# A two-layer hybrid decoder step on one core: where the low halves of the next weights and of the later prompt rows are made

## The chip, the core and the metric

The kernel runs on one core of one Trainium2 chip. The metric is the device time of one execution in microseconds (us); lower is better. A core has five engines that run their own instruction streams: TensorE (PE in the rows, with its weight loads as PEld), VectorE (DVE), ScalarE (ACT), GpSimd (POOL) and SyncE (SP, which here only issues DMAs). They meet through semaphores.

## The reference, cut to what matters

Two layers, each of them one mixer over 2048 prompt rows and 32 sample rows (8 sequences of 4 tokens) of width 1024, in float32:

```python
for l in range(DEPTH):                                    # DEPTH = 2
    h = rms_norm(x, norm_g[l])
    p = h @ w_in[l]                                       # 1024 x 3328, columns split as
    qa, ka, va, ga, qb, kb, vb, gb = split(p)             # 512 128 128 512 | 4 x 512
    attn = sliding-window attention of qa, ka, va with sinks   # 8 heads of 64, 2 kv heads, window 128
    ret  = rms_norm(retention of qb, kb, vb)              # 4 heads of 128, chunks of 128
    x = x + concat(silu(ga) * attn, silu(gb) * ret) @ w_out[l]
```

The outputs are x for prompt and sample, and the new key, value and retention states.

## The kernel before, in words

**Two halves in place of float32.** TensorE multiplies in float16. Each float32 factor is scaled by a power that keeps it in range and split into a high half, hi = f16(x * s), and a low half, lo = f16(x * s - hi). A product is the sum of three matmuls (hi*hi, hi*lo, lo*hi). The high half of a weight chunk is made by ACT (`w_high`, the ACTIVATE at line 1692), the low half by DVE in one instruction (`w_low`, lines 916 to 920: multiply by the scale, subtract the high half, write float16). For the rows of x it is the same: `p_high` (line 1894) on ACT, `p_low` (line 1348) on DVE.

**Stages.** A layer has four stages, named by their weights: A (attention: q, k, v and its gate, 1280 columns), B0 and B1 (retention, two heads each, 1024 columns) and O (the output product). Each stage walks over 17 steps: the sample rows and 16 tiles of 128 prompt rows. The weights of a stage lie in one of two SBUF slots, `w_a` (A, B1) and `w_b` (B0, O). While one stage runs, the weights of the next are loaded by POOL's DMAs into the other slot as float32, and its halves are written over them in place: the halves of chunk (k, c) end 512 words below where its raw values begin, so the low half of a chunk must be made before ACT may write the high half of the next one. That is the wait of `w_high` on the semaphore `w_lo` in front of line 1692. In stage A the next weights are B0's: 8 rows k of 128, each in two chunks c of 128x512.

**Stage A step by step.** Step s projects tile s on PE (three parts: q with 512 columns, k and v with 256, gate with 512) and at the same time takes tile t = s-1 through scores and softmax and tile u = s-2 through the product with the values. On PE (`a_step`, `a_work`) the order is: the first three quarters of part 0, the transposes of q and k of t, the rest of part 0, half of part 1, the scores of t (`a_S`, line 637), the rest of part 1, values product of u for kv group 0 (`a_PV`, line 677), three quarters of part 2, values product of u for group 1, the rest. On DVE (`a_step`, lines 1427 to 1488): low halves of q and k (`a_lo`, lines 1020 and 1022; the scores wait for them), landing of q (`a_land_q`, line 960), low halves of the probabilities of u, group 1 (`a_plo`, line 1053), the masks and maxima of both groups of t (line 1091), landing of k (line 976), the four mixed heads of group 0 and of group 1 (line 1166) with the small instructions of the norm of tile s woven between them, its rotation (lines 1002 to 1014), the gate (line 1034), and the low half of the probabilities of t, group 0 (`a_plo`, line 1048). The probabilities go through a transposing DMA issued by SP (`prob_T`, line 2192) before `a_PV` can use them, and there is one buffer for each group, so the masks of the next tile wait for the transpose of this one.

**Where the low halves stand.** In steps 8 to 15 of stage A DVE's `a_step` has `w_low(L, "B0", k, 0)` in the middle of the norm's small instructions and `w_low(L, "B0", k, 1)` at the end. ACT's `a_step` has `w_high(k, 0)` before it lands k and v, and `w_high(k, 1)` between the exponentials of group 0 and those of group 1.

**The prompt rows of layer 0.** The normalised rows h of tiles 1 to 16 are not all made before the first step. Tiles 1 to 7 are made in the prologue and steps 0 and 1. Tiles 8 to 16 are made late (`late_h`): in step c of 4 to 12, ACT makes the high half of tile c+4, DVE its low half (`p_low(c + 4)`, at the end of the step), and SP sends both through a transposing DMA into `hT` (`p_T`, line 2184), queued on SP behind the `prob_T` of that step. The raw rows lie in `hT` itself, at the place their transpose will take. In steps 4 to 6 DVE also takes the absolute maxima of the B0 weights (`w_absmax`, line 902), in step 6 the overall maximum, and in step 7 the scales (`w_scale`).

**POOL.** It loads weights (`load_weights`, lines 510 to 518) and reduces one column across partitions (`share_max`, line 2086). In `attend` (lines 2094 to 2105) it waits for one piece of stage A, loads the eight rows of B0's weights, and reduces the maximum in step 6. In layer 1 DVE, ACT, PE and SP run the middle steps in hardware loops; in layer 0 DVE's and ACT's steps 8 to 15 are written out, since `late_h` differs by step.

Of the kernel before, what the change touches and what calls it, by code (L numbers as in the profile page):

```python
# [197 lines left out]
def trunk(nc, x_prompt, x_sample, cache_k, cache_v, state_ret, w_in, w_out, norm_g, q_g, k_g, sinks,  # L198
          rope_ap, rope_as, rope_bp, rope_bs, mask_a, mask_s, decay, decay_s, cols, ident,
          y_p, y_s, nk_p, nv_p, nst_p, nk_s, nv_s, nst_s, mixed):  # L200
    with ExitStack() as ctx:
# [3 lines left out]
        def sem(name):  # L205
            return ctx.enter_context(nc.semaphore(name))
# [130 lines left out]
        h_planes = nc.dram_tensor("h_planes", (ROWS, 2 * D_MODEL), F16).ap()  # L337
        alone_count = sem("alone_count")

        ch_wm, ch_ws = sem("chain_w_max"), sem("chain_w_scale")  # L340
        ch_an, ch_asm, ch_amx = sem("chain_a_norm"), sem("chain_a_softmax"), sem("chain_a_mix")
        ch_ams, ch_bo, ch_om = sem("chain_a_mix_sample"), sem("chain_b_out"), sem("chain_o_scale")
# [109 lines left out]
        def x_of(n):  # L452
            return px[:, n % RING, :] if n < PRO else hx[:, :, (n - 1) * 64:n * 64]
# [405 lines left out]
        def _(v):  # L859
# [56 lines left out]
            def w_low(L, kind, k, c):  # L916

                v.wait_ge(w_hi, wparts(L, kind, k, c) + 1)
                V.scalar_tensor_tensor(out=w16(kind, k, c, 1), in0=raw(L, kind, k, c), scalar=w_gs[:, run(k, 1)],  # L919
                                       in1=w16(kind, k, c, 0), op0=ALU.mult, op1=ALU.subtract).then_inc(w_lo, 1)  # L920
# [423 lines left out]
            def p_low(n):  # L1344

                r = NS if n == 0 else P
                v.wait_ge(x_hi, n + 1)
                V.scalar_tensor_tensor(out=xh_of(n, 1)[0:r], in0=x_of(n)[0:r], scalar=py[0:r, n:n + 1],
                                       in1=xh_of(n, 0)[0:r], op0=ALU.mult, op1=ALU.subtract).then_inc(x_lo, 1)
# [52 lines left out]
            def layer(L, last):  # L1402
# [21 lines left out]
                    a_softmax(L, s - 1, 1)  # L1424
                    gate("A", L, s, 2, A_W, A_W + 2 * KV_W)

                def a_step(s, k=None):

                    t, u = s - 1, s - 2
                    if u.sample:  # L1430
# [23 lines left out]
                    if not u.sample:  # L1454
# [6 lines left out]
                        a_norm_link(s, ch, 2)  # L1461
                        a_mix_head(u, 0, 3).then_inc(a_mx, 1)
                        a_norm_link(s, ch, 3)
                        if k is not None:
                            w_low(L, "B0", k, 0)
                        a_norm_link(s, ch, 4)
                        a_norm_link(s, ch, 5)
                        a_mix_open(L, u, 1, m1)
# [10 lines left out]
                        a_rotate(L, s, ch)  # L1479
                        gate("A", L, s, 2, A_W, A_W + 2 * KV_W)  # L1480
                        a_plo(L, t, 0)
                        if k is not None:
                            w_low(L, "B0", k, 1)
                    else:
                        a_norm(s, ch)
                        a_rotate(L, s, ch)
# [4 lines left out]
                def late_h(c):  # L1491

                    if c == 0:
                        p_rstd(1)
                        p_low(4)
                        p_low(5)
                    if c == 1:
                        p_low(6)
                        p_low(7)
                    if c in (3, 4):  # L1500
                        p_rstd(c - 1)
                    if 4 <= c <= 12:
                        p_low(c + 4)

                for c in range(CVA):
                    if c < 2:
# [9 lines left out]
                        w_top(L, "B0")  # L1516
                    if c == 7:
                        w_scale(L, "B0")
                if L == 0:
                    for c in range(CVA, CVA + KT):  # L1520
                        a_step(Step(c), c - CVA)
                        late_h(c)
                else:
                    with v.Fori(0, KT // 2) as i:
                        for c in (0, 1):
                            a_step(Step(CVA + c, i), c + 2 * i)
                for c in range(CVA + KT, STEPS):
                    a_step(Step(c))

# [551 lines left out]
        def _(pool):  # L2081
# [9 lines left out]
            pool.sem_inc(st_out, 64)  # L2091
            share_max(0, "A")

            def attend(L):

                for c in range(STEPS):
                    if c == 2 and L == 0:
                        for p in range(2):
                            pool.wait_ge(h_in[p], 16 * (PRO // 2))
                    if c == 2:  # L2100
                        pool.wait_ge(dve_piece, L * PIECES + PIECE0["A"] + 1)
                    if c in (2, 3):
                        load_weights(G, "B0", L, range(4 * c - 8, 4 * c - 4))
                    if c == 6:
                        share_max(L, "B0")

            def layer(L, last):
                attend(L)
# [341 lines left out]
```

## Time and profile before

| | |
|---|---|
| runs | 1910.03, 1909.19, 1908.5 us; median 1909.19 |
| the profiled execution | 1908.13 us, of which its span is 1906.3 us |
| mean granted TensorE clock | 0.984 |
| busy share of the span | PE 93%, PEld 50%, DVE 72%, ACT 43%, POOL 4% |
| instructions | PE 11512, DVE 4744, ACT 1901, POOL 108 |
| stage A of layer 0 | about 65 to 400 us of the span |
| stage A of layer 1 | about 1005 to 1320 us |

The profile shows one execution. A group's row gives its busy time, the mean duration in ns, and the idle time of the engine before it with what ended that. A row of the timeline gives start, duration and, in square brackets, the idle time before it and its releaser. Engines overlap the tail of one instruction with the start of the next, so the time that an instruction costs its engine is the distance to the start of the next one, which is up to 0.09 us less than its duration; the chain of waits counts that distance.

### The profile page before, as it was taken

How to read it: one execution, taken by the hardware profiler on the slowest of the kernel's cores; microseconds unless marked ns; L12 is line 12 of the kernel's file. 1: busy time of each engine (PE TensorE's matmuls, PEld its weight loads, DVE VectorE, ACT ScalarE, POOL GpSimd, SP SyncE). 2: the span in 40 equal slices, each digit the busy share in tenths (PEclk: the TensorE clock that was granted, in tenths of full speed). 3: DMA queues.
4: the chain of work that ended last, by engine and by line, in shares of the span. 5: the costliest groups of instructions: out<-in, count | busy, mean ns of one | idle time of the engine just before them, and what ended most of it. 6: DMA issues, size and time to landing. Idle time of an engine off the chain costs nothing.

```text
span 1906.3 us, 35688 instructions
## 1 busy us (share of the span) xinstructions
PE 1770.3 (93%) x11512; PEld 961.3 (50%) x11512; DVE 1379.1 (72%) x4744; ACT 820.7 (43%) x1901; POOL 68.5 (4%) x108
## 2 busy tenths in 40 slices
PE   0778899999999999989998989999999999999999
PEld 0345555555555555543445555555555555555444
DVE  4768999987665666678885899998766666667442
ACT  2556566652443334432443556665344333442010
POOL 3010000000000000011001000000100000000000
PEclk9898999999999999999999999999999999999999
DMA  5874455466114311179894454554611133115774
GB/s 152 207 185 73 88 105 112 107 119 159 30 33 123 81 31 33 33 207 269 251 267 135 80 100 95 110 115 86 186 31 33 46 111 81 32 32 142 207 207 143
DMA packets 419519, 220.91 MB, mean 116 GB/s; under 512 B 360257, under 2 KB 391169, under 8 KB 419265
## 3 DMA queue, kind: packets, MB, share of 16 engines
q1 hardware_dynamic: 346336, 168.41, 36.4%
q0 software_dynamic: 9728, 35.66, 5.7%
q10 hardware_dynamic: 63360, 15.74, 4.9%
q8 instruction: 41, 0.67, 0.1%
q14 instruction: 54, 0.43, 0.1%
HBM read 88.75 MB, written 49.68 MB: 73 GB/s over the span
## 4 chain that ended last, share of the span: by engine, by line
PE 55%; DVE 23%; DMA 8%; ACT 5%; issue 4%; SPq 2%; DVEq 0%; ACTq 0%; POOL 0%
PE PB L547 23%; PE PA L547 22%; DMA r<-r 6%; DVE r L1091 2%; DVE r L1048 2%; DVE w_mx L902 1%; PE S L701 1%; PE OB L721 1%; PE S L737 1%; PE OB L728 1%; DVE mix L1166 1%; DVE r L1053 1%; DVE w_b L919 1%; ACT w_a L1762 1%; DVE w_a L919 1%
## 5 line engine op out<-in xcount | busy, mean ns | idle before, releaser
L547 PE MATMUL PB<-w_a,hT 128*128 128x512 f16 (+1 forms) x1920 | 406.1, 365 | 0.0
L547 PE MATMUL PA<-w_a,hT 128*128 128x512 f16 (+1 forms) x1920 | 401.4, 360 | 0.6 <-DVE land L1034 0.6
L547 PEld LDWEIGHTS PB<-w_a,hT 128*128 (+1 forms) x1920 | 187.0, 99 | 184.4 <-issue 18.9
L547 PEld LDWEIGHTS PA<-w_a,hT 128*128 (+1 forms) x1920 | 185.3, 98 | 177.0 <-issue 5.6
L1840 ACT ACTIVATE w_a<-land 128x1024 uint16<-128x1024 uint16 x60 | 63.4, 1057 | 294.2 <-DVE land L1206 281.9
L547 PE MATMUL PA<-w_b,r 128*128 128x512 f16 x768 | 175.6, 387 | 11.7 <-DMA r<-r 9.5
L547 PE MATMUL PB<-w_b,hT 128*128 128x512 f16 x768 | 176.0, 380 | 1.3 <-DVE r L1195 1.3
L547 PE MATMUL PA<-w_b,hT 128*128 128x512 f16 x768 | 173.7, 382 | 0.0
L547 PE MATMUL PB<-w_b,r 128*128 128x512 f16 x768 | 171.4, 379 | 2.3 <-DVE r L1313 1.1
L1762 ACT ACTIVATE r<-r,nm,unqk 128x256 f32<-128x256 f32 x192 | 112.6, 588 | 46.1 <-DVE sd L1104 46.1
L547 PEld LDWEIGHTS PA<-w_b,r 128*128 128x128 f16 x768 | 75.6, 99 | 106.8 <-DMA r<-r 11.2
L547 PEld LDWEIGHTS PB<-w_b,r 128*128 128x128 f16 x768 | 74.8, 98 | 93.2 <-DVE r L1319 2.1
L547 PEld LDWEIGHTS PA<-w_b,hT 128*128 (+1 forms) x768 | 74.9, 98 | 85.8 <-issue 4.2
L547 PEld LDWEIGHTS PB<-w_b,hT 128*128 (+1 forms) x768 | 74.7, 98 | 84.5 <-DVE r L1195 1.4
L1862 ACT ACTIVATE r<-r,minv 128x1024 f16<-128x1024 f32 (+1 forms) x34 | 39.0, 1148 | 145.5 <-DVE minv L1280 137.9
L1034 DVE SCALAR_TENSOR_TENSOR land<-land,PB 128x256 f32<-128x256 f32 (+2 forms) x50 | 25.3, 506 | 105.5 <-ACT land L1814 100.4
L1034 DVE SCALAR_TENSOR_TENSOR land<-land,PA 128x256 f32<-128x256 f32 (+3 forms) x52 | 26.7, 513 | 89.1 <-ACT land L1814 86.8
L1834 ACT ACTIVATE r<-w_a 128x1024 uint16<-128x1024 uint16 x60 | 82.1, 1368 | 20.6 <-DMA w_a<-w_a 20.6
L573 PE MATMUL PA<-w_a,hT 128*32 128x256 f16 (+1 forms) x336 | 22.0, 342 | 54.7 <-DVE w_a L919 53.8
L1319 DVE SCALAR_TENSOR_TENSOR r<-PB,mdd,r 128x512 f32<-128x512 f32 x32 | 23.9, 748 | 64.7 <-PE PB L547 64.4
L1692 ACT ACTIVATE w_b<-w_b,w_gs (+1 forms) x64 | 46.4, 725 | 23.1 <-DVE w_b L919 16.1
L1294 DVE SCALAR_TENSOR_TENSOR r<-r,minv 128x1024 f16<-128x1024 f32 (+1 forms) x34 | 43.4, 1278 | 17.2 <-ACT r L1862 17.1
(265 smaller groups left out, 2875.5 us busy)
## 6 DMA issues: line engine op xcount, KB each, us to landing
out<-r SPq DMA_DIRECT2D x40, 512.0 KB, 4.7
r<-mixed SPq DMA_DIRECT2D x32, 512.0 KB, 4.2
w_b<-in_w_in POOLq DMA_DIRECT2D x16, 512.0 KB, 8.8
mixed<-mix SPq DMA_DIRECT2D x32, 256.0 KB, 2.0
mixed<-mix SPq DMA_DIRECT2D x64, 128.0 KB, 1.8
w_a<-in_w_in POOLq DMA_DIRECT2D x16, 512.0 KB, 8.2
w_b<-in_w_out POOLq DMA_DIRECT2D x16, 512.0 KB, 7.8
r<-in_x_prompt SPq DMA_DIRECT2D x16, 512.0 KB, 4.4
```

The source lines that it names most:

```text
L547: last = nc.tensor.matmul(out[0:s.rows, 0:n], lhs, w16(ph, k, p, wpart), start=(k == 0 and part == 0 and wpart == 0), stop=(k == KT - 1 an ...
L919: V.scalar_tensor_tensor(out=w16(kind, k, c, 1), in0=raw(L, kind, k, c), scalar=w_gs[:, run(k, 1)], in1=w16(kind, k, c, 0), op0=ALU.mult, ...
L1034: V.scalar_tensor_tensor(out=th, in0=th, scalar=1.0, in1=src, op0=ALU.add, op1=ALU.mult).then_inc(dve_piece, 1)
L1048: V.scalar_tensor_tensor(out=ph16[0][:, 1, :], in0=r1[:, 1536:2560], scalar=P_TOP, in1=ph16[0][:, 0, :], op0=ALU.mult, op1=ALU.subtract).t ...
L1091: return V.tensor_tensor_reduce(out=prob_q[g][h // 2][:, h % 2 * 256:h % 2 * 256 + 256], in0=(SS, XX)[g][h // 2][:, (h % 2) * 256:(h % 2) ...
L1294: V.scalar_tensor_tensor(out=m[0:r, 1, :], in0=mxt[0:r, b, :], scalar=minv[0:r, b:b + 1], in1=m[0:r, 0, :], op0=ALU.mult, op1=ALU.subtract ...
L1319: V.scalar_tensor_tensor(out=x, in0=bank("O", s, p)[0:r, :], scalar=mdd[0:r, b:b + 1], in1=x, op0=ALU.mult, op1=ALU.add).then_inc(dve_piec ...
L1692: A.activation(w16(kind, k, c, 0), raw(L, kind, k, c), ACT.Copy, scale=w_gs[:, run(k, 1)]).then_inc(w_hi, 1)
L1762: A.activation(x, x, ACT.Exp, scale=unqk[:, 0:1], bias=nm[:, g, h:h + 1], accum_out=rsum[:, g, h:h + 1])
L1834: last = A.activation(qkT.bitcast(U16).rearrange("p (n e) -> p e n", e=2), plT, ACT.Copy)
L1840: A.activation(pl, land[:, lpar(ph, s), 0:512].bitcast(U16).rearrange("p (n e) -> p e n", e=2), ACT.Copy).then_inc(b_pl, 1)
L1862: A.activation(mh_of(s)[0:r, 0, :], mxt[0:r, b, :], ACT.Copy, scale=minv[0:r, b:b + 1]).then_inc(o_hi, 1)
```

## The change

In stage A the low halves of B0's weights (both layers) and of the late prompt tiles 8 to 16 (layer 0) leave DVE and go to POOL. There each is made by two instructions: a `tensor_scalar` that scales the raw values where they lie, and, after a wait for its own semaphore, a `tensor_tensor` that subtracts the high half and writes float16. DVE's steps 8 to 15 of layer 0 become a hardware loop as in layer 1. POOL loads the B0 weights in two groups of four rows, the second after three more pieces of stage A. The low halves of the other stages stay on DVE, and ACT's and SP's programs are unchanged.

```diff
+        w_pp = sem("w_scaled_in_place")
+        x_ps = sem("x_scaled_in_place")
...
# DVE
-                def a_step(s, k=None):
+                def a_step(s):
...
                         a_norm_link(s, ch, 3)
-                        if k is not None:
-                            w_low(L, "B0", k, 0)
                         a_norm_link(s, ch, 4)
...
                         a_plo(L, t, 0)
-                        if k is not None:
-                            w_low(L, "B0", k, 1)
...
                     if c in (3, 4):
                         p_rstd(c - 1)
-                    if 4 <= c <= 12:
-                        p_low(c + 4)
...
-                if L == 0:
-                    for c in range(CVA, CVA + KT):
-                        a_step(Step(c), c - CVA)
-                        late_h(c)
-                else:
-                    with v.Fori(0, KT // 2) as i:
-                        for c in (0, 1):
-                            a_step(Step(CVA + c, i), c + 2 * i)
+                with v.Fori(0, KT // 2) as i:
+                    for c in (0, 1):
+                        a_step(Step(CVA + c, i))
...
# POOL
+            def w_low(L, kind, k, c):
+
+                pool.wait_ge(w_hi, wparts(L, kind, k, c) + 1)
+                n = (L * KT + k) * len(CH[kind]) + c
+                x = raw(L, kind, k, c)
+                G.tensor_scalar(x, x, w_gs[:, k:k + 1], None, ALU.mult).then_inc(w_pp, 1)
+                pool.wait_ge(w_pp, n + 1)
+                G.tensor_tensor(w16(kind, k, c, 1), x, w16(kind, k, c, 0), ALU.subtract).then_inc(w_lo, 1)
+
+            def p_low(n):
+
+                pool.wait_ge(x_hi, n + 1)
+                x = x_of(n)
+                G.tensor_scalar(x, x, py[:, n:n + 1], None, ALU.mult).then_inc(x_ps, 1)
+                pool.wait_ge(x_ps, n - PRO + 1)
+                G.tensor_tensor(xh_of(n, 1), x, xh_of(n, 0), ALU.subtract).then_inc(x_lo, 1)
+
             def attend(L):
 
-                for c in range(STEPS):
-                    if c == 2 and L == 0:
-                        for p in range(2):
-                            pool.wait_ge(h_in[p], 16 * (PRO // 2))
-                    if c == 2:
-                        pool.wait_ge(dve_piece, L * PIECES + PIECE0["A"] + 1)
-                    if c in (2, 3):
-                        load_weights(G, "B0", L, range(4 * c - 8, 4 * c - 4))
-                    if c == 6:
-                        share_max(L, "B0")
+                if L == 0:
+                    for p in range(2):
+                        pool.wait_ge(h_in[p], 16 * (PRO // 2))
+                pool.wait_ge(dve_piece, L * PIECES + PIECE0["A"] + 1)
+                load_weights(G, "B0", L, range(4))
+                pool.wait_ge(dve_piece, L * PIECES + PIECE0["A"] + 4)
+                load_weights(G, "B0", L, range(4, KT))
+                if L == 0:
+                    for n in range(PRO, PRO + 3):
+                        p_low(n)
+                share_max(L, "B0")
+                if L == 0:
+                    p_low(PRO + 3)
+                for k in range(KT):
+                    for c in range(2):
+                        w_low(L, "B0", k, c)
+                    if L == 0 and PRO + 4 + k < STEPS:
+                        p_low(PRO + 4 + k)
```

Here PRO is 8, KT is 8, CVA is 8 and STEPS is 17.

## Rows read from the trace of the kernel before

**Rows 1.** The page's second part, the span in 40 slices of 47.7 us.
```profile
DVE  4768999987665666678885899998766666667442
...
PEclk9898999999999999999999999999999999999999
```
**Rows 2.** DVE's timeline (start, duration): landing of q, first instruction but three of a step.
```profile
155.34 0.75 DVE L960 SCALAR_TENSOR_TENSOR land<-PA,cs_A,qk_g 128x512 f32<-128x512 f32 x1
...
239.17 0.72 DVE L960 SCALAR_TENSOR_TENSOR land<-PA,cs_A,qk_g 128x512 f32<-128x512 f32 x1
...
328.03 0.72 DVE L960 SCALAR_TENSOR_TENSOR land<-PB,cs_A,qk_g 128x512 f32<-128x512 f32 x1
...
378.59 0.72 DVE L960 SCALAR_TENSOR_TENSOR land<-PA,cs_A,qk_g 128x512 f32<-128x512 f32 x1
...
1156.36 0.72 DVE L960 SCALAR_TENSOR_TENSOR land<-PA,cs_A,qk_g 128x512 f32<-128x512 f32 x1
...
1296.19 0.72 DVE L960 SCALAR_TENSOR_TENSOR land<-PA,cs_A,qk_g 128x512 f32<-128x512 f32 x1
```
**Rows 3.** The chain that ended last, layers 0 and 1 (start, us, what).
```profile
265.50 0.67 DVE w_b L919
...
272.50 1.20 DVE r L1348
...
1224.97 4.72 DMA r<-r
```
**Rows 4.** ACT's timeline around the two high halves of one step, layer 0.
```profile
256.67 0.71 ACT L1692 ACTIVATE w_b<-w_b,w_gs 128x512 f16<-128x512 f32 x1
...
266.25 0.72 ACT L1692 ACTIVATE w_b<-w_b,w_gs 128x512 f16<-128x512 f32 x1 [0.72 <-DVE w_b L919]
```
**Rows 5.** PE's timeline, layer 0: first part-1 matmuls of steps 14 and 15.
```profile
361.07 1.47 PE L547 MATMUL PA<-w_a,hT 128*128 128x256 f16 x12
...
377.52 1.47 PE L547 MATMUL PB<-w_a,hT 128*128 128x256 f16 x12
```
**Rows 6.** PE's timeline: the scores at the end of steps 4, 5 and 6.
```profile
177.86 0.40 PE L637 MATMUL S<-kT_hi,r 64*128 64x256 f16 x2 [4.51 <-DVE r L1022]
...
199.46 0.28 PE L637 MATMUL S<-kT_hi,r 64*128 64x256 f16 x2 [2.60 <-DVE r L1022]
...
220.60 0.40 PE L637 MATMUL S<-kT_hi,r 64*128 64x256 f16 x2 [3.00 <-DVE r L1022]
```
**Rows 7.** Windows (us, then busy PE, PEld, DVE, ACT, POOL; PEclk; DMA share; GB/s).
```profile
180.00:182.00 2.00, 2.00 (x13) 1.17 (x10) 2.00 (x11) 0.00 (x0) 0.00 (x0) 0.50 0.13 26
...
222.00:224.00 2.00, 2.00 (x18) 1.16 (x15) 2.00 (x8) 0.00 (x0) 0.00 (x0) 0.50 0.00 0
```
**Rows 8.** Waits (total us, times, longest): stretch 176 to 241, then 241 to 328.
```profile
DVE mix L1166 <- PE TK L677: 3.8, 3, 1.9
...
PE S L637 <- DVE r L1022: 3.8, 4, 1.0
```
**Rows 9.** DVE's groups by form, 241 to 410 us (busy us, mean ns).
```profile
L1048 DVE SCALAR_TENSOR_TENSOR r<-r 128x1024 f16<-128x1024 f32 x10 | 12.2, 1218 | 0.0
L919 DVE SCALAR_TENSOR_TENSOR w_b<-w_b,w_gs 128x512 f16<-128x512 f32 x16 | 11.9, 745 | 0.0
...
L1348 DVE SCALAR_TENSOR_TENSOR r<-hT,py,r 128x1024 f16<-128x1024 f32 x5 | 6.4, 1278 | 0.0
...
L1014 DVE TENSOR_TENSOR land<-r 128x80 f32<-128x80 f32 x9 | 2.1, 235 | 0.0
```
**Rows 10.** Timeline at the start of layer 1, POOL and PE.
```profile
1005.68 5.96 POOL L518 DMA_DIRECT2D w_b<-in_w_in  x8 [104.31 <-DVE r L1319]
...
1020.29 0.28 PE L587 MATMUL TK<-eye,land 32*64 32x32 f32 x4 [2.65 <-DVE land L1014]
```
**Rows 11.** SP's own timeline, layer 0: two transposing DMAs in their order.
```profile
256.11 2.67 SPq L2184 DMA_TRANSPOSE hT<-r  x1
259.73 1.32 SPq L2192 DMA_TRANSPOSE r<-r  x1
```

## The prediction

> **What bounds the kernel now.** I read the page's slices first, because the change touches only stage A, about a third of the span. DVE's digits there are 8 and 9 in layer 0 (slices 4 to 8) and again around layer 1's stage A, while in the retention stages they are 6 and 7 [rows 1]. So DVE is fullest exactly where the change takes work off it. The landings of q then give the length of a step [rows 2]. In layer 0 steps 4 to 7 take (239.17 - 155.34) / 4 = 20.96 us each, steps 8 to 12 (which have both kinds of low half) (328.03 - 239.17) / 5 = 17.77, steps 13 to 15 (weights only) (378.59 - 328.03) / 3 = 16.85. In layer 1 steps 8 to 15 take (1296.19 - 1156.36) / 8 = 17.48.
>
> What would PE need by itself? From the first part-1 matmuls of step 14 to those of step 15 it had no wait: 377.52 - 361.07 = 16.45 us at the full clock [rows 5]. That is the floor of a step.
>
> The chain says who sets each step. In layer 0 it runs through DVE, with the weight low halves (0.67 us each; the second of a step costs the same) and the row low half (1.20 us) on it [rows 3], and PE waits up to 1.0 us a step for DVE before the scores [rows 8]. In layer 1 it is a loop: masks, softmax, the first weight low half, ACT's high half and exponentials, gate, low half of the probabilities, then 4.72 us of transposing DMA [rows 3] before the next masks may use the buffer. Only the first of the two weight low halves is on that loop. Layer 0 shows the same link: ACT waited 0.72 us for DVE's `w_low` before the second high half [rows 4].
>
> Steps 4 to 6 of layer 0 have something more. PE waits 4.51, 2.60 and 3.00 us for DVE before the scores [rows 6], and behind the first and the third of them windows show a granted clock of 0.50, the lower level, 1.2 GHz [rows 7]. The waits of up to 1.0 us in steps 8 to 12 [rows 8] have no such dip behind them. DVE later pays: it waits 3.8 us in three places for PE's values product, 1.9 of them behind the longest gap [rows 8].
>
> **The change part by part.** The sum is made against the profiled execution, 1908.13 us; the median is 1.06 us above it, which I add at the end.
>
> *Row low halves leave DVE in steps 4 to 7.* 4 x 1.20 = 4.8 us off a full engine [rows 3]. The gaps of steps 5 and 6 shrink to 1.4 and 1.8 us; I take it that the clock then holds, as behind the 1.0 us gaps, and DVE's two later waits, 3.8 - 1.9 = 1.9 us [rows 8], go. Step 4 keeps a gap of 3.3 and its dip. Gain 6.7 us.
>
> *Both kinds leave DVE in steps 8 to 15, layer 0.* DVE gets back 2 x 0.67 + 1.20 = 2.54 us in five steps and 1.34 in three, 16.7 us; PE's floor lets through (378.59 - 239.17) - 8 x 16.45 = 7.8.
>
> *Layer 1.* The loop loses one low half: 8 x 0.7 = 5.6 us, under the floor's 139.83 - 131.6 = 8.2. The second one is beside the DMA, and gives nothing while the DMA covers it.
>
> *What POOL's instructions cost.* No row shows POOL at arithmetic. Nearest are DVE's single instructions over the same tiles, 0.75 us for 128x512 and 1.28 for 128x1024 [rows 9]; that is the lower end. The upper end at which POOL would still keep ACT's pace comes from ACT's two high halves: 266.25 - 0.72 - 257.38 = 8.15 us for two instructions, 4.1 each [rows 4]. I take DVE's durations for each of the two instructions, the nearest row. Then POOL works 4 x 0.75 + 2 x 1.28 = 5.56 us in a step with both kinds and 3.0 in one with weights only; its own time is hidden by 17 us of step.
>
> *What it costs DVE.* POOL now reads SBUF beside DVE. No row shows the two side by side, so the cost to DVE is between nothing and all of POOL's time. Should they share a path, DVE's instructions with two SBUF inputs are those exposed. In the 169 us from 241 to 410 fifteen groups are of that kind, from line 1048 with 12.2 us to line 1014 with 2.1 [rows 9], 72.7 us together, 0.43 of the stretch and 0.48 of what is left once the moved instructions are gone. I take 0.45 of POOL's time as lost to DVE. Steps 8 to 12: 0.45 x 5.56 = 2.50 against 2.54 won, nothing. Steps 13 to 15: 1.35 against 1.34, nothing. Layer 1: the second pair runs right behind ACT's second high half, beside the norm and the rotation, which are on the loop; 0.45 x 1.5 = 0.68 against 0.7, nothing. Steps 4 to 7: a pair of 2.56 us, but DVE is then partly in `w_absmax` with one input; half a us each, 2.0. Ends of this term: 0, and all of POOL's time added.
>
> The Trainium skill, SBUF — State Buffer, section Who interferes with whom, speaks against this change: a DVE instruction with two SBUF inputs and a GpSimd instruction that reads SBUF exclude each other for a whole instruction, whoever is second. No row here shows that. GPSIMD Engine Reference, section 3.1, gives a GpSimd `tensor_tensor` 1.96 times DVE's duration; with a `tensor_scalar` near DVE's own that makes 1.5 on average, an estimate, and the sum would be that of the second rival.
>
> *Small parts.* DVE's new loop in layer 0 adds register work; layer 1 has it and steps within 0.6 us of layer 0's; I take 0, at most 2 us in all. The four later loads of B0's weights in layer 1: all eight are issued at 1005.68 [rows 10]; four would now start when k of step 1 has landed, near 1028, and are needed in step 5, some 90 us later: hidden. Emptier DMAs at 1006 to 1020 win nothing, since PE waits there for DVE's rotation until 1020.29 [rows 10]. In layer 0 the piece has long come when the prologue's transposes release POOL. `share_max` in layer 0 stands behind `p_low(10)`, and DVE asks for it a step of 21 us later: hidden. SP's `p_T` now waits for POOL, with `prob_T` queued behind it: third rival.
>
> Sum: -4.8 - 1.9 + 2.0 = -4.7: 1903.4 us, by the median 1904.5. By itself this case reaches from 1899 to 1911.
>
> **The rivals.**
> *No contention.* POOL and DVE don't disturb each other. Then 6.7 + 7.8 + 5.6 = 20.1 us come off: 1889.1. For it: DVE is the engine in front, and PE's floor is a full us below the steps. Against: POOL's reads have to come from somewhere. Chance 0.20.
> *POOL's instructions hold DVE up for longer than the moved work took.* Place: beside `a_plo` and beside norm and rotation. Break-even is where POOL's instructions last 1.2 times DVE's. At 1.5 times: steps 8 to 12, 5 x (3.75 - 2.54) = 6.1; steps 13 to 15, 3 x (2.03 - 1.34) = 2.1; layer 1, 8 x (1.01 - 0.7) = 2.5; steps 4 to 7, 3.0 - 6.7 = -3.7. Together +7.0: 1916.2. At twice, +19: 1928. For it: nearly half of DVE's time is exposed. Chance 0.30.
> *SP is held up.* `p_T` takes 2.67 us of SP and the next `prob_T` follows at 259.73 [rows 11]. If POOL ends a row's low half 2 us later against DVE's plan than DVE did, that `prob_T` and PE's product behind it come later by as much, beyond the 1.3 us a step of room above the floor: with DVE's gain lost too, five steps at about 1.5 us, 1912. Chance 0.07.
> That the change does nothing to the moved work is excluded: the instructions are gone from DVE. Remainder 0.03.
>
> **How the numbers follow.** Forecast 0.40, rivals 0.20, 0.30, 0.07. A measurement of this kernel tells 0.2%, 3.8 us, from no change, so faster is below 1905.4. Half of the forecast's own range and a little of the second rival's lie there, with the first rival: 0.20 + 0.22 + 0.05 = 0.47. Slower, above 1913: most of the second rival, 0.30 with the third. The rest, 0.23, is no change. The range has to hold the first rival's value and the second at 1.6 times: 1888 to 1920.
>
> **What would show it right or wrong.** Landings of q in layer 0: steps 5 and 6 near 19 to 20 us, without a clock of 0.50 behind them; steps 8 to 12 near 17.7. If these are near 16.5, the first rival holds; above 18, the second. In the groups, line 1048 keeps its 1218 ns [rows 9] if nothing is shared, and it and the other two-input lines are longer on average if DVE waits inside them. POOL's `tensor_scalar` and `tensor_tensor` rows give the missing durations. A PE wait for the DMA before line 677 that grows by over 1 us in steps 8 to 12 is the third rival. The prediction is wrong in its reasons if the time moves in B0, B1 or O.

## The result, and the profile after

| | before | after |
|---|---|---|
| runs | 1902.85 to 1910.03 us, median 1908.85 (4) | 1921.85 to 1931.72 us, median 1929.95 (4) |
| the profiled execution, its span | 1908.13, 1906.3 us | 1931.28, 1929.5 us |
| mean granted clock | 0.984 | 0.978 |

The changed kernel takes 1.0102 times as long, with a 95% interval of 1.0075 to 1.0128. It is slower by about 20 us, where 1904.5 was forecast.

The slices of the page after answer to [rows 1]. POOL's digits are those that the change adds (3 to 5 in layer 0's stage A, up to 3 in layer 1's).

```profile
DVE  4768999987666666678885799999666666667442
...
POOL 3011345401000000011001002331100000000000
PEclk9798999999999999999998999999999999999999
```

DVE is as full as before, with less work to do. The landings of q, of DVE's timeline after, answer to [rows 2] (start, duration):

```profile
155.73 0.75 DVE L962 SCALAR_TENSOR_TENSOR land<-PA,cs_A,qk_g 128x512 f32<-128x512 f32 x1
...
240.34 0.72 DVE L962 SCALAR_TENSOR_TENSOR land<-PA,cs_A,qk_g 128x512 f32<-128x512 f32 x1
...
343.57 0.71 DVE L962 SCALAR_TENSOR_TENSOR land<-PB,cs_A,qk_g 128x512 f32<-128x512 f32 x1
...
397.48 0.75 DVE L962 SCALAR_TENSOR_TENSOR land<-PA,cs_A,qk_g 128x512 f32<-128x512 f32 x1
...
1175.61 0.72 DVE L962 SCALAR_TENSOR_TENSOR land<-PA,cs_A,qk_g 128x512 f32<-128x512 f32 x1
...
1319.73 0.75 DVE L962 SCALAR_TENSOR_TENSOR land<-PA,cs_A,qk_g 128x512 f32<-128x512 f32 x1
```

Steps 4 to 7 of layer 0 take (240.34 - 155.73) / 4 = 21.15 us (before 20.96), steps 8 to 12 (343.57 - 240.34) / 5 = 20.65 (before 17.77), steps 13 to 15 17.97 (before 16.85), and layer 1's steps 8 to 15 (1319.73 - 1175.61) / 8 = 18.02 (before 17.48). In us that is +0.8, +14.4, +3.4 and +4.3. The last landing comes 1319.73 - 1296.19 = 23.5 us later than before, and the span is 23.2 longer. The four stretches make 22.8 of it, most of that in the five steps with both kinds of low half. What else moved nearly cancels: step 1 of layer 1 is 6.3 us longer, steps 2 to 7 there are 1.5 shorter, and the time between the two stages A is 4.4 shorter (see One load group).

What POOL's instructions last is in POOL's groups by form over the whole span (busy us, mean ns):

```profile
L2090 POOL TENSOR_SCALAR w_b<-w_b,w_gs 128x512 f32<-128x512 f32 x32 | 55.7, 1740 | 180.0 <-ACT w_b L1683 180.0
L2092 POOL TENSOR_TENSOR w_b<-w_b 128x512 f16<-128x512 f32 x32 | 39.4, 1230 | 2.7
L2098 POOL TENSOR_SCALAR hT<-hT,py 128x1024 f32<-128x1024 f32 x9 | 26.3, 2920 | 101.4 <-ACT r L1885 101.4
L2100 POOL TENSOR_TENSOR r<-hT,r 128x1024 f16<-128x1024 f32 x9 | 19.6, 2183 | 0.7
```

A step with both kinds holds 2 x (1.74 + 1.23) + 2.92 + 2.18 = 11.0 us of POOL's work, where the prediction took 5.56.

Now the place where it costs. First POOL's timeline in step 10 of layer 0, then DVE's rows of the same time:

```profile
283.72 1.63 POOL L2092 TENSOR_TENSOR w_b<-w_b 128x512 f16<-128x512 f32 x1
292.16 1.56 POOL L2090 TENSOR_SCALAR w_b<-w_b,w_gs 128x512 f32<-128x512 f32 x1 [6.81 <-ACT w_b L1683]
293.81 1.16 POOL L2092 TENSOR_TENSOR w_b<-w_b 128x512 f16<-128x512 f32 x1
296.21 2.98 POOL L2098 TENSOR_SCALAR hT<-hT,py 128x1024 f32<-128x1024 f32 x1 [1.24 <-ACT r L1885]
299.27 2.15 POOL L2100 TENSOR_TENSOR r<-hT,r 128x1024 f16<-128x1024 f32 x1
```
```profile
284.25 1.12 DVE L1118 TENSOR_TENSOR rr<-rsum,es 128x4 f32<-128x4 f32 x1
...
292.26 0.61 DVE L883 TENSOR_TENSOR rt<-rs 128x10 f32<-128x10 f32 x1
292.99 0.15 DVE L885 TENSOR_TENSOR rt<-rt,ss 128x10 f32<-128x10 f32 x1
...
293.92 1.07 DVE L887 SCALAR_TENSOR_TENSOR rs<-rt,rs 128x10 f32<-128x10 f32 x1
...
296.60 0.95 DVE L1015 TENSOR_TENSOR land<-r 128x80 f32<-128x80 f32 x1
...
298.22 1.21 DVE L1050 SCALAR_TENSOR_TENSOR r<-r 128x1024 f16<-128x1024 f32 x1
...
299.36 2.08 DVE L1118 TENSOR_TENSOR rr<-rsum,es 128x4 f32<-128x4 f32 x1
```

A sum of 128x4 values takes 2.08 us and ends at 301.44, with POOL's `tensor_tensor` (301.42). The mean of its line before, from 241 to 410, was 157 ns, and after it is 1008. Line 887 shows the same: 15 of its instructions in the two layers last about 1.07 us instead of 0.16, and each ends within 0.04 us of the end of a 128x512 `tensor_tensor` of POOL. The instructions are counted as busy while they stand still, which is why DVE's digits didn't fall. Of the 128x512 `tensor_scalar` only the beginning does this: L883 is released 0.70 us after its start, and L885 then runs in 0.15 us although the `tensor_scalar` goes on for 0.7 us more. Added up, what these five rows last beyond their usual 0.15 to 0.24 is (1.12 - 0.16) + (0.61 - 0.16) + (1.07 - 0.17) + (0.95 - 0.24) + (2.08 - 0.16) = 4.9 us, against the 2.54 us that left DVE.

Over all five steps, counted as what DVE's instructions last beyond their median durations in the write-only kernel below, DVE's stalls are 4.9 us a step too. What remains of them after the 2.54, 2.4 us, doesn't quite make the 2.88 by which a step grew; the other half a us is not assigned.

PE meets it mainly in two places. Its waits after, from 241 to 343 us (total us, times, longest), answer to the second line of [rows 8]:

```profile
PE S L603 <- DVE land L1016: 7.2, 5, 1.7
...
PE S L639 <- DVE r L1024: 4.5, 4, 1.1
```

The wait before the scores has grown a little. The one before the transposes of q and k, for the end of DVE's rotation (line 1016), is new: before the change no such wait of PE is listed in steps 8 to 12. The stalls in the norm's small instructions and in the rotation come out there. Another 4.5 us of waits stand before the values product (line 679), where before there were 0.3.

### The profile page after: what moved, and what is told of

It reads as the page before. It is cut to its first block, busy times and chain, and to the rows that moved or that the text cites. A ratio compares the mean times of both kernels' runs of the same rounds, so it can differ in the third digit from the quotient of the medians.

```text
span 1929.5 us, 35982 instructions
## 1 busy us (share of the span) xinstructions
PE 1777.0 (92%) x11512; PEld 962.9 (50%) x11512; DVE 1400.7 (73%) x4703; ACT 819.1 (42%) x1901; POOL 210.3 (11%) x190
## 4 chain that ended last, share of the span: by engine, by line
PE 55%; DVE 25%; DMA 7%; issue 5%; SPq 3%; ACT 2%; DVEq 1%; ACTq 0%; POOL 0%
PE PB L549 23%; PE PA L549 22%; DMA r<-r 5%; DVE r L1093 2%; DVE r L1050 2%; PE S L703 1%; PE OB L723 1%; DVE land L1004 1%; PE S L739 1%; DVE mix L1168 1%; PE OB L730 1%; DVE rs L887 1%; DVE w_mx L904 1%; DVE rt L883 1%; DVE r L1055 1%
## 5 line engine op out<-in xcount | busy, mean ns | idle before, releaser
L2090 POOL TENSOR_SCALAR w_b<-w_b,w_gs 128x512 f32<-128x512 f32 x32 | 55.7, 1740 | 180.0 <-ACT w_b L1683 180.0
```

Source lines behind the costliest of these rows:

```text
L2090: G.tensor_scalar(x, x, w_gs[:, k:k + 1], None, ALU.mult).then_inc(w_pp, 1)
```

## The experiments

All kernels after the change's own are compared with runs of the kernel before on the same chip, whose median lay between 1907.3 and 1909.7 us. Step lengths are from the landings of q, as above, each of one profiled execution.

| kernel | L0, 4 to 7 | 8 to 12 | 13 to 15 | L1, 8 to 15 | median us | ratio (95%) |
|---|---|---|---|---|---|---|
| before | 20.96 | 17.77 | 16.85 | 17.48 | 1908.85 | 1 |
| after | 21.15 | 20.65 | 17.97 | 18.02 | 1929.95 | 1.0102 (1.0075 to 1.0128) |
| write only | 19.09 | 16.45 | 16.61 | 16.72 | 1883.3 | 0.9869 (0.9845 to 0.9892) |
| side work | 22.10 | 21.60 | 17.79 | 18.51 | 1941.75 | 1.0160 (1.0126 to 1.0194) |
| weights only | 20.95 | 18.70 | 17.89 | 17.96 | 1918.86 | 1.0055 (1.0034 to 1.0077) |
| rows only | 21.08 | 18.22 | 17.20 | 17.74 | 1914.52 | 1.0020 (1.0001 to 1.0040) |
| early rows | 20.73 | 17.76 | 16.81 | 17.54 | 1905.74 | 0.9994 (0.9968 to 1.0020) |
| scale only | 20.77 | 17.14 | 17.06 | 17.19 | 1901.51 | 0.9964 (0.9940 to 0.9988) |
| subtract only | 21.49 | 20.41 | 17.89 | 17.97 | 1926.13 | 1.0077 (1.0045 to 1.0109) |
| one load group | 20.98 | 20.65 | 17.98 | 18.17 | 1930.21 | 1.0105 (1.0074 to 1.0136) |
| timed | 20.91 | 17.51 | 16.72 | 16.95 | 1896.96 | 0.9949 (0.9918 to 0.9979) |
| timed later | 20.75 | 16.53 | 16.72 | 17.10 | 1900.09 | 0.9960 (0.9946 to 0.9973) |
| timed by layer | 20.98 | 16.53 | 16.71 | 17.02 | 1896.69 | 0.9937 (0.9908 to 0.9966) |

### Write only: the relief without the reading

```diff
-                G.tensor_scalar(x, x, w_gs[:, k:k + 1], None, ALU.mult).then_inc(w_pp, 1)
-                pool.wait_ge(w_pp, n + 1)
-                G.tensor_tensor(w16(kind, k, c, 1), x, w16(kind, k, c, 0), ALU.subtract).then_inc(w_lo, 1)
+                G.memset(w16(kind, k, c, 1), 0.0).then_inc(w_lo, 1)
```
The same is done in `p_low`.

> The changed kernel, but POOL makes no low half: in the place of its two instructions stands one memset of the low half's place, which reads nothing. The low halves are left out (zero), all waits and handovers stay. Port theory (a DVE instruction with two SBUF inputs stands still while a POOL instruction reads SBUF): the stalls inside DVE's small instructions go, steps 8 to 15 of stage A fall to 16.5 to 16.9 us in both layers, steps 5 and 6 of layer 0 to under 20, and the time is 1886 to 1895 us, faster than before. Hardware-loop theory (DVE's loop in layer 0 costs what was lost): steps 8 to 15 of layer 0 stay above 17.8 us, layer 1 falls, total 1905 to 1915. Handover theory (ACT, SP and PE wait for a low half that comes late): as the port theory here, since a memset is short; the next run tells them apart.

Measured: 1883.3 us, below the range given. Steps 8 to 12 take 16.45 us, which is exactly the floor of PE. So what left DVE is worth what the prediction said (steps 4 to 7 7.5 us, 8 to 15 of layer 0 7.35, layer 1 6.1; predicted 6.7, 7.8 and 5.6), DVE's hardware loop in layer 0 costs nothing that shows, and POOL's writing held up nothing in these steps. The profiled execution is 25.7 us shorter than that of before; some 5 us of this lie outside the stages A (2.9 between them, 2.4 behind the last landing), and no run says why.

The prediction's account of steps 5 and 6 can be read here too. PE's timeline before the scores, and windows at the same distance behind as those of [rows 7]:

```profile
196.73 0.28 PE L639 MATMUL S<-kT_hi,r 64*128 64x256 f16 x2 [1.40 <-DVE r L1024]
...
215.61 0.28 PE L639 MATMUL S<-kT_hi,r 64*128 64x256 f16 x2 [2.08 <-DVE r L1024]
```
```profile
199.00:201.00 2.00, 1.88 (x33) 1.33 (x32) 2.00 (x11) 0.62 (x2) 0.00 (x0) 1.00 0.40 79
...
217.00:219.00 2.00, 1.84 (x26) 1.43 (x25) 2.00 (x9) 0.37 (x2) 0.00 (x0) 1.00 0.06 14
```

The gaps shrank to 1.40 and 2.08 us, and the clock stayed at its upper level behind both. Step 4 kept a gap of 3.31 us and its dip.

### Side work: the reading without the relief

The kernel before, with the same two kinds of POOL instruction at the same times on a table that nobody else needs then:

```diff
+                G.tensor_scalar(t, t, ones[:, 0:1], None, ALU.mult).then_inc(sem_, 1)
+                pool.wait_ge(sem_, n + 1)
+                G.tensor_tensor(t, t, ones[:, 0:1].broadcast_to([P, m]), ALU.mult).then_inc(side, 1)
```

> The kernel before, DVE still makes every low half, but POOL does two reading instructions of the same sizes beside it (a tensor_scalar by 1.0 in place and a two-input tensor_tensor on a table that stage A does not use), started by the same high halves. Nobody waits for them until stage A is over. Port theory: DVE is held up as in the changed kernel but has won nothing back: steps 8 to 12 of layer 0 take 21 to 23 us, steps 13 to 15 about 18.5, layer 1 18 to 19, total 1935 to 1955. Handover theory: nothing waits for POOL, so 1909 within 4 us.

Measured: 1941.75 us, steps 8 to 12 at 21.60 us, both inside their ranges; steps 13 to 15, at 17.79 us, stay below the 18.5 given. No engine waits for this work until long after it, so a handover between engines is not what costs. POOL's two reading instructions beside DVE are enough: the cost is there by their presence alone, and with the write-only kernel it is the reading that brings it.

### Weights only, rows only, early rows

In the first DVE keeps the rows' low halves, in the second the weights', and in the third POOL has the rows' low halves of steps 4 to 6 alone. The diff is the third's, against the kernel before:

```diff
-                    if 4 <= c <= 12:
+                    if 7 <= c <= 12:
                         p_low(c + 4)
...
+                    if L == 0 and 4 <= c <= 6:
+                        p_low(c + 4)
```

> Only the low halves of the B0 weights are on POOL, those of the prompt rows are back on DVE (whose steps in layer 0 are written out again). Port theory: POOL's two pairs cost DVE some 2.3 us a step against 1.34 won, so steps 8 to 15 of layer 0 take about 1 us more than before, layer 1 0.5 more (as changed), steps 4 to 7 as before: 1918 to 1924. If the rows alone cause the loss: 1909 or less.

> Only the low halves of the late prompt rows are on POOL, those of the weights are back on DVE. Port theory: the row pair costs DVE some 2.6 us a step against 1.20 won, so steps 8 to 12 take 19 to 19.5 us against 17.8 before, steps 4 to 7 within 1.5 us in sum of before, layer 1 as before: 1914 to 1920. If the weights alone cause the loss: 1905 or less.

> The kernel before with only the rows' low halves of steps 4, 5 and 6 on POOL; all else stays on DVE. Theory (in these steps POOL's pair stands mostly beside the maxima, which have one input, but costs about what it gives): 1906 to 1911 us, no change. Rival (the gaps of PE in steps 4 to 6 shrink and the clock holds, as predicted): 3 to 5 us off, 1903 to 1906 us.

Measured: 1918.86, 1914.52 and 1905.74 us. The first two are inside the ranges given, though steps 8 to 12 of rows only, at 18.22 us, stay below the 19 given. The third lies just inside the rival's range, but its interval holds 1, and the rival's reason is not seen: windows at 201 to 203 and 222 to 224 us show the clock at 0.50 as before. Each kind costs by itself, the rows barely (their interval begins at 1.0001, and layer 1, where rows only has the code of before, took 0.26 us a step more in the profiled execution). The two costs, about 9 and 5 us against the same runs of before, don't make up the 21 of the whole change. In steps 8 to 12 they are 0.93 and 0.45 us a step against 2.88 for both. What DVE's instructions last beyond their usual durations there, counted as above, is 2.4 us a step with the weights, 1.6 with the rows and 4.9 with both; less the 1.34, 1.20 and 2.54 us that left DVE this is 1.05, 0.44 and 2.4. So both kinds together hold more of DVE than the two by themselves.

In rows only the 1.6 us stand in two places. POOL's rows and DVE's around the end of step 9:

```profile
272.73 3.43 POOL L2097 TENSOR_SCALAR hT<-hT,py 128x1024 f32<-128x1024 f32 x1 [12.77 <-ACT r L1893]
276.24 2.14 POOL L2099 TENSOR_TENSOR r<-hT,r 128x1024 f16<-128x1024 f32 x1
```
```profile
273.36 1.60 DVE L920 SCALAR_TENSOR_TENSOR w_b<-w_b,w_gs 128x512 f16<-128x512 f32 x1
...
277.20 1.20 DVE L1124 TENSOR_SCALAR rr<-rr,cs_A 128x4 f32<-128x4 f32 x1
```

The second of them (0.22 us by itself) has one tile of 128x4 and a column as its factor, and is not among the prediction's fifteen groups; it ends with POOL's `tensor_tensor`.

Steps 4 to 6 show the account in small. After the change POOL's and DVE's timelines at the end of step 5:

```profile
191.98 2.90 POOL L2098 TENSOR_SCALAR hT<-hT,py 128x1024 f32<-128x1024 f32 x1 [14.58 <-ACT r L1885]
194.96 2.13 POOL L2100 TENSOR_TENSOR r<-hT,r 128x1024 f16<-128x1024 f32 x1
```
```profile
192.17 1.07 DVE L1016 TENSOR_TENSOR land<-r 128x80 f32<-128x80 f32 x1
...
193.76 1.21 DVE L1050 SCALAR_TENSOR_TENSOR r<-r 128x1024 f16<-128x1024 f32 x1
194.90 3.46 DVE L904 TENSOR_REDUCE w_mx<-w_b 128x1 f32<-128x1024 f32 x3
```

The `tensor_tensor` lies wholly beside `w_absmax`, which has one input and loses nothing (3.46 us for three). The `tensor_scalar` keeps L1016 for 1.07 instead of 0.24. Of the 1.20 us won, 0.83 is lost, and 0.37 is left. PE's wait before the scores shrank by 0.36 (PE's timeline after, in steps 5 and 6, against 2.60 and 3.00 in [rows 6]):

```profile
199.40 0.28 PE L639 MATMUL S<-kT_hi,r 64*128 64x256 f16 x2 [2.24 <-DVE r L1024]
...
220.17 0.28 PE L639 MATMUL S<-kT_hi,r 64*128 64x256 f16 x2 [2.64 <-DVE r L1024]
```

And the clock fell behind both as before (windows after; columns as in [rows 7]; before, a window from 201 to 203 shows 0.50 too):

```profile
201.00:203.00 2.00, 2.00 (x12) 1.20 (x9) 2.00 (x8) 0.00 (x0) 0.00 (x0) 0.50 0.37 70
...
222.00:224.00 2.00, 2.00 (x14) 1.17 (x9) 2.00 (x10) 0.00 (x0) 0.00 (x0) 0.50 0.00 0
```

### Scale only, subtract only: which of the two instructions holds DVE

```diff
# scale only
                 G.tensor_scalar(x, x, w_gs[:, k:k + 1], None, ALU.mult).then_inc(w_pp, 1)
                 pool.wait_ge(w_pp, n + 1)
-                G.tensor_tensor(w16(kind, k, c, 1), x, w16(kind, k, c, 0), ALU.subtract).then_inc(w_lo, 1)
+                G.memset(w16(kind, k, c, 1), 0.0).then_inc(w_lo, 1)
...
# subtract only
-                G.tensor_scalar(x, x, w_gs[:, k:k + 1], None, ALU.mult).then_inc(w_pp, 1)
-                pool.wait_ge(w_pp, n + 1)
                 G.tensor_tensor(w16(kind, k, c, 1), x, w16(kind, k, c, 0), ALU.subtract).then_inc(w_lo, 1)
```

> Left out: the subtraction. POOL scales the raw values in place as in the changed kernel, and then fills the low halves with zeros by a memset, which reads nothing. Theory (POOL's tensor_scalar keeps DVE's two-input instructions waiting only in the first 0.7 us of 1.56, or 1.3 us of 2.9; the tensor_tensor keeps them waiting for all of its length): stalls of 1 to 2 us a step, under the 2.54 us that left DVE; steps 8 to 12 of layer 0 at 16.5 to 17.0 us, in all 1886 to 1895 us. Rival (both instructions hold DVE by the same share of their length; the tensor_scalar is then 57 per cent of the cost): steps 8 to 12 near 18.0 us, in all 1900 to 1912 us.

> Left out: the scaling, so the low halves are those of unscaled values. POOL does only the tensor_tensor that reads two tiles. Theory (it is the tensor_tensor that holds DVE): stalls near 3.9 us a step against 2.54 won; steps 8 to 12 of layer 0 at 18.5 to 19.5 us, in all 1912 to 1922 us. Rival (both instructions hold DVE by the same share of their length): 43 per cent of the stalls, steps 8 to 12 near 17.3 us, in all 1895 to 1903 us.

Measured: 1901.51 us with the scaling alone, a gain over the kernel before but above the range of the theory and at the low end of the rival's; its steps 8 to 12, 17.14 us, lie between the two as well, nearer the theory's 17.0. Line 1050 did grow here, to 1.74 us on average in these steps, since POOL's scaling of the rows now started only 0.4 to 0.6 us ahead of it (2.0 us in step 10 of the changed kernel). With the subtraction alone it is 1926.13 us, outside both ranges on the theory's side, with steps 8 to 12 at 20.41 us, nearly the 20.65 of the whole change, and steps 13 to 15 and layer 1 as in the whole change. The `tensor_tensor` is 43% of POOL's time and brings nearly all of the loss. I had expected 3.9 us of stalls a step from it; the groups of DVE in steps 8 to 12, against those of the write-only kernel, add up to 3.6 us a step, and the step is longer by 20.41 - 16.45 = 4.0. One of them, POOL's row and then DVE's of the same step:

```profile
316.75 2.20 POOL L2096 TENSOR_TENSOR r<-hT,r 128x1024 f16<-128x1024 f32 x1 [2.89 <-ACT r L1885]
```
```profile
316.73 0.24 DVE L1015 TENSOR_TENSOR land<-r 128x80 f32<-128x80 f32 x1
316.89 2.17 DVE L1016 TENSOR_TENSOR land<-r 128x80 f32<-128x80 f32 x1
```

Where it begins decides what it costs: this L1016 is the end of the rotation, for which PE waits before its transposes.

### One load group

```diff
-                load_weights(G, "B0", L, range(4))
-                pool.wait_ge(dve_piece, L * PIECES + PIECE0["A"] + 4)
-                load_weights(G, "B0", L, range(4, KT))
+                load_weights(G, "B0", L)
```

> The changed kernel with POOL's eight loads of B0's weights issued in one group, as before the change. Theory (the loads are hidden either way, and the long step 1 of layer 1 is an episode of the halved clock that kernels with either order of loads show): no difference from the changed kernel, 1925 to 1932 us. Rival (the split loads cost the 6.3 us of layer 1's step 1): 1920 to 1924 us.

Measured: 1930.21 us, and step 1 of layer 1 takes 32.75 us, to the hundredth that of the changed kernel. In the kernel before it took 26.47, with the clock at 1.00 where after the change a window shows 0.50:

```profile
1038.50:1041.50 3.00, 3.00 (x5) 1.44 (x5) 0.00 (x0) 0.63 (x2) 0.00 (x0) 0.50 0.02 5
```

The split loads are not the cause: weights only has them, and a step 1 of 26.47; rows only has the loads of before, and 29.45. Why the clock is low there in some kernels was not settled. In the changed kernel's own account the stages between the two make up for 4.4 of its 6.3 us (637.99 us from the last landing of layer 0 above to the landing of step 1 of layer 1, against 642.37).

### Timed: POOL's reading put beside one-input work

If only the overlap with DVE's two-input instructions costs, POOL must be told when to start. Against weights only:

```diff
+                if c == 0:
+                    pool.wait_ge(a_vl, L * TILES + k + 6)
                 G.tensor_scalar(x, x, w_gs[:, k:k + 1], None, ALU.mult).then_inc(w_pp, 1)
                 pool.wait_ge(w_pp, n + 1)
+                if c == 0:
+                    pool.wait_ge(a_sm, 2 * (L * STEPS + k + 7) + 1)
+                else:
+                    pool.wait_ge(qk_hi, L * TILES + k + 8)
                 G.tensor_tensor(w16(kind, k, c, 1), x, w16(kind, k, c, 0), ALU.subtract).then_inc(w_lo, 1)
```

> Weights' low halves on POOL, rows' low halves on DVE as before, and three added waits on POOL: the first tensor_scalar of a step starts with DVE's landing of v, the first tensor_tensor with the mixed heads' scales of the next tile, the second tensor_tensor with the next landing of q, where DVE reads PSUM or has one input. Theory (only an overlap with DVE's two-input instructions costs): most of the 5 us lost by the untimed kernel with weights alone on POOL come back and more; steps 8 to 12 of layer 0 near 17 us, in all 1895 to 1905 us. Rival (POOL's reading costs DVE the same wherever it stands, or ACT's second high half comes too late through the added waits): 1915 to 1925 us.

(The waits stand at the low half of v, where the masks of group 0 begin, at the masks of group 1, and at the high half of q.) Measured: 1896.96 us, some 20 us under the same kernel without the waits (0.9949 against 1.0055 of before) and the first kernel with the whole computation to beat the one before (interval 0.9918 to 0.9979). Steps 8 to 12 still took 17.51, above the 17 expected. POOL's row and DVE's tell why:

```profile
303.79 1.16 POOL L2105 TENSOR_TENSOR w_b<-w_b 128x512 f16<-128x512 f32 x1 [4.53 <-ACT r L1742]
```
```profile
303.82 1.16 DVE L1118 TENSOR_TENSOR rr<-rsum,es 128x4 f32<-128x4 f32 x1
```

The second `tensor_tensor` starts 0.03 us ahead of the small sum. So it was moved once more:

```diff
-                    pool.wait_ge(qk_hi, L * TILES + k + 8)
+                    pool.wait_ge(qk_lo, L * TILES + k + 8)
```

> As the timed kernel, but POOL's second tensor_tensor of a step waits for DVE's low half of q instead of the high half, so that it stands beside the landing of q (one input from PSUM) and not on the small sum of the softmax. Theory (the 1.0 us in which that sum stood still in every step is a stall behind this tensor_tensor, and ACT has 2.4 us of room before the next high half is missed): that row returns to 0.16 us, steps 8 to 12 of layer 0 at 16.5 to 16.8 us, layer 1's at 16.5 to 16.9, in all 4 to 8 us less than the timed kernel: 1889 to 1894 us. Rival (the later low half holds up ACT's next high half and with it the landing of k and v): no better than the timed kernel, 1896 to 1902 us.

```profile
288.53 1.16 POOL L2105 TENSOR_TENSOR w_b<-w_b 128x512 f16<-128x512 f32 x1 [5.78 <-DVE r L1024]
```
```profile
287.31 0.15 DVE L1118 TENSOR_TENSOR rr<-rsum,es 128x4 f32<-128x4 f32 x1
288.38 0.72 DVE L962 SCALAR_TENSOR_TENSOR land<-PB,cs_A,qk_g 128x512 f32<-128x512 f32 x1
289.02 0.68 DVE L966 TENSOR_REDUCE ss<-r 128x8 f32<-128x512 f32 x1
```

The sum is back at 0.15 us, and the landing of q (one factor from PSUM) and the reduction run beside POOL in their usual 0.72 and 0.68. Steps 8 to 12 take 16.53 us, 0.08 above the floor. That part of the expectation holds, the time doesn't: 1900.09 us, outside the 1889 to 1894 of the theory and inside the rival's range. The rival's mechanism is not seen, though (ACT waits 1.2 us in all for POOL in five steps). Layer 1 is no faster (17.10 against 16.95), and the stages between take 645.81 us where the timed kernel has 639.45, with 0.87 and 0.79 of the clock in two windows there, where the timed kernel shows 1.00 at the same distance from its last landing:

```profile
871.60:881.60 10.00, 2.72 (x13) 1.04 (x11) 5.23 (x6) 1.15 (x2) 2.03 (x3) 0.87 1.19 114
881.60:891.60 10.00, 9.27 (x36) 3.88 (x37) 6.60 (x17) 2.30 (x2) 0.00 (x0) 0.79 1.03 300
```

The last kernel takes the later wait in layer 0 alone (`qk_hi if L else qk_lo`).

> The second tensor_tensor waits for DVE's low half of q in layer 0 and for ACT's high half in layer 1. Theory (the two layers' stages A keep the steps that each wait gave by itself, 16.5 us in steps 8 to 12 of layer 0 and near 17.0 in layer 1, and what the whole kernel gave besides is the clock in the stages between, which no wait of stage A sets): stages A 13 us shorter than before in all, the time between them within 5 us of before's 642 us, in all 1892 to 1900 us. Rival (the later wait of layer 0 costs time in the stages behind it): the time between the stages at 646 us or more again, in all 1899 to 1903 us.

Measured: 1896.69 us, 0.9937 with 0.9908 to 0.9966, inside the theory's range. The stages A (16.53, 16.71 and 17.02 us a step) are as each wait gave them, and the time between them is 643.83 us. This is the best version found; among the three timed ones the medians differ by less than their intervals can part.

## Why the prediction was wrong

**The relief of DVE** was right, as the write-only kernel shows: 7.5, 7.35 and 6.1 us, 21 in all, where 6.7, 7.8 and 5.6, 20.1 in all, were predicted. The gaps of steps 5 and 6 shrank to 1.40 and 2.08 us (1.4 and 1.8 predicted), and the clock held behind them.

**The share of POOL's time that DVE loses** was right for the steps with both kinds: 0.45 taken, 4.9 us of POOL's 11.0 in step 10 found, which is 0.45 again. But that is an average over two unlike instructions, and its agreement is in part luck: counted in the same way, DVE's stalls are 2.1 us of POOL's 5.97 in steps 13 to 15, 0.35, and 1.75 of 6.0 in layer 1, 0.29 (where the prediction charged only one of the two pairs). Nor did it fall on the fifteen groups by their time. What stood still was mostly the small ones among them (L1118, L887, L883, L1015 after the change), which happen to be next when POOL starts; line 1048, named as the sign, kept its 1.21 us.

**What POOL's instructions cost is the step that failed.** "I take DVE's durations for each of the two instructions, the nearest row" gave 5.56 us a step; the trace shows 11.0, 1.98 times as much. With that size in the prediction's own formula the loss in steps 8 to 12 is 0.45 x 11.0 = 4.95 against 2.54 won, +2.4 us a step where +2.9 was measured; in steps 13 to 15 0.45 x 5.94 = 2.7 against 1.34, +1.3 where +1.1 was measured; in layer 1 0.45 x 2.97 = 1.3 against 0.7, +0.6 where +0.5 was measured. The second rival's value "at twice" was 1928 us; the kernel takes 1929.95 (that sum has steps 4 to 7 gain 2.7 us where they lost 0.8, and step 1 of layer 1 and the stages between are not in it, so the nearness is in part chance). It was given for POOL at twice DVE's durations, and its break-even at 1.2 times should have moved the forecast. To take the lower of two bounds for a price on another engine, because it was the nearest row in shape, was the choice that decided.

The Trainium skill, GPSIMD Engine Reference, section 3.1, which I weighed and set aside, has a GpSimd `tensor_tensor` at 1.96 times DVE's duration. Here it ran at 1.16 us undisturbed against DVE's 0.75 for the single instruction that it helps to replace, 1.5 times. The `tensor_scalar`, which I had taken as near DVE's own, was the longer of the two: 1.56 us undisturbed, 2.1 times DVE's. The rule that the Trainium skill gives in SBUF — State Buffer, section Who interferes with whom, by which the two exclude each other for a whole instruction, holds here for the `tensor_tensor`: L1118 ended with it in step 10. For the `tensor_scalar` the measurement differs, since it let DVE's L885 pass after its first 0.70 us.

**Steps 4 to 7** were predicted to gain 4.7 us with the clock back, and lost 0.8. The stall was 0.83 us, not half a us, the gaps of 2.24 and 2.64 us were still followed by the clock's lower level (those of 1.40 and 2.08 us in the write-only kernel were not), and in step 7 the tiny `w_gs` instruction (line 930) stood still behind POOL's `tensor_tensor` of the row, for 1.87 us instead of 0.23. PE's wait before the scores is 2.09 us there, where before it was 0.49, and the clock fell behind it as well (0.50 in a window from 242 to 244 us). Since it held behind the 2.08 us of the write-only kernel, the length of the gap alone doesn't decide; what does is open. The row of line 930:

```profile
236.46 1.87 DVE L930 TENSOR_SCALAR w_gs<-g_cur,w_s 128x8 f32<-128x8 f32 x1
```

**The small parts** at zero were right: the loop (write only is at the floor with it) and the split loads (one load group). SP was not held up: PE's waits in steps 8 to 12 list no DMA, before or after, so the third rival is out. In the profile nearly all of the time moved in the stages A, as said; the 4.4 us by which the stages between them were shorter are of the size by which that time differs between kernels that are the same there (637.99 and 644.68 us for the changed kernel and its version with one load group).

## What to carry to other kernels

Before work goes from VectorE to GpSimd, ask what DVE does at the moment when GpSimd starts: a `tensor_tensor` there that begins ahead of a DVE instruction with two SBUF inputs keeps it until its own end, however small the DVE instruction is, and a DVE `tensor_scalar` with a column as its factor can be kept too. The same work cost nothing beside DVE's reductions, its masks and the landings from PSUM, so a wait that does nothing but choose the moment can turn a loss into a gain (here from 1.0055 to 0.9949 of the time before). When the sign of a forecast turns within the bounds of a price that no row shows, the lower bound is no forecast: the break-even (here 1.2 times the lower bound, against 1.98 measured) is what the chances must be set around.

## What the runs showed of the hardware that was not expected

- On POOL a `tensor_scalar` with a column as its factor is slower than a `tensor_tensor` of the same size (here float32 in place, against float32 less float16 into float16): 1.56 against 1.16 us for 128x512, 2.90 against 2.13 for 128x1024.
- Its hold on DVE's small instructions ends early (0.70 us after the start of the 128x512 one, about 1.3 us after that of the 128x1024 one), that of the `tensor_tensor` with its end. A memset of POOL held no two-input instruction (steps at PE's floor). In scale only, though, the `w_gs` instruction (line 930) took 0.67 us instead of 0.23 and ended with POOL's memset of 128x1024 (235.17 and 235.14).
- POOL waits as well: 1.63 us instead of 1.16 for the `tensor_tensor` at 283.72.
- A DVE `tensor_scalar` whose factor is a column in SBUF can stand still too (line 930 above; L1125 after the change, at 241.57, for 1.01 us instead of 0.22; L1124 in rows only, 1.20 in each of five steps); `w_absmax`, the landing of q and its reduction never did in the rows shown.
